# Writing out the loops of four engines as straight code in a two-layer transformer trunk

## What is computed

```python
for l in range(DEPTH):                                   # DEPTH = 2
    need_ctx = l < DEPTH - 1
    mod  = silu(c)     @ w_mod[l] + b_mod[l]             # 6 rows of 1024
    modc = silu(c_ctx) @ w_mod[l] + b_mod[l]
    h, hc = modulated rms_norm of x, of xc
    p = (h or hc) @ w_in[l]                              # q, k, v, gates of three mixers
    y = sigmoid(g0) * (retention(p) @ w_ret_o) \
      + sigmoid(g1) * (latent_attention(p) @ w_mla_o) \
      + sigmoid(g2) * (grouped_attention(p) @ w_gqa_o)
    x = x + mod[2] * (y @ w_out)
    h2 = modulated rms_norm of x
    a, b = split(h2 @ w_ffn_in[l]);  x = x + mod[5] * ((silu(a) * b) @ w_ffn_out[l])
    # the same for the context stream xc, only where need_ctx
return rms_norm(x, g_final)
```

## Time and profile before

| | before |
|---|---|
| runs | 3406.63, 3413.54, 3417.59 us; median 3413.54 |
| the profiled execution | 3408.35 us, its span 3406.2 us |
| instructions in the trace | 49718 |
| TensorE matmul busy | 3200.3 us (94%), 18760 matmuls |
| VectorE, ScalarE, GpSimd busy | 44%, 36%, 12% |
| loads of function tables on ScalarE | 96, of 1.283 us each |
| mean granted TensorE clock | 0.977 of full speed |

### The profile page before, as it was taken

One profiled execution on the slowest core, in us unless ns is written; L12 is line 12 of the kernel. 1 busy time (PEld: TensorE's weight loads), 2 busy tenths in 40 slices (PEclk: granted clock), 3 DMA queues, 4 the chain that ended last, 5 costly groups with the idle time before them and its releaser, 6 DMA issues.

```text
span 3406.2 us, 49718 instructions
## 1 busy us (share of the span) xinstructions
PE 3200.3 (94%) x18760; PEld 2716.6 (80%) x18760; DVE 1512.8 (44%) x2047; ACT 1241.8 (36%) x1777; POOL 397.4 (12%) x304
## 2 busy tenths in 40 slices
PE   6999999999999989999999988998999899899998
PEld 5788888899888878788888867887788787678886
DVE  5555524454436533422222255554455456443334
ACT  3344432444434432221211234444355444432222
POOL 0011100111102201000100100111011112010001
PEclk9999999999999999999999988999999999899999
DMA  4222132111242243123232332222222242322222
GB/s 187 75 70 73 68 124 76 63 62 60 76 150 66 67 139 128 55 91 119 68 122 88 123 124 85 76 73 82 89 76 73 73 133 81 118 80 99 93 98 99
DMA packets 100921, 315.17 MB, mean 93 GB/s; under 512 B 11088, under 2 KB 21456, under 8 KB 100816
## 3 DMA queue, kind: packets, MB, share of 16 engines
q1 hardware_dynamic: 55872, 202.40, 18.0%
q10 hardware_dynamic: 44944, 111.32, 9.7%
HBM read 283.79 MB, written 29.88 MB: 92 GB/s over the span
## 4 chain that ended last, share of the span: by engine, by line
PE 52%; DVE 4%; issue 3%; ACT 2%; POOL 0%; DMA 0%; ACTq 0%; DVEq 0%; POOLq 0%
PE ps L1443 49%; PE ps L1531 1%; PE ps L1558 1%; DVE wl L921 1%; ACT wh L441 0%; POOL ptl L1425 0%; DVE tmp L931 0%; DVE hl L1096 0%; PE ps L1572 0%; DVE tmp L1087 0%; DMA xz<-xspill 0%; PE ps L1467 0%; ACT prob L492 0%; ACTq L674 0%; PE ps L1501 0%
## 5 line engine op out<-in xcount | busy, mean ns | idle before, releaser
L1443 PE MATMUL ps<-hh,wh 128*128 128x512 f32 x2768 | 831.7, 361 | 35.3 <-DVE wl L921 15.5
L1443 PE MATMUL ps<-hh,wl 128*128 128x512 f32 x2768 | 814.0, 354 | 0.0
L1443 PE MATMUL ps<-hl,wh 128*128 128x512 f32 x2768 | 813.5, 354 | 0.0
L921 DVE TENSOR_TENSOR wl<-raw,wh 128x1024 fp32r<-128x1024 f32 x364 | 489.0, 1344 | 515.3 <-ACT wh L441 486.4
L1443 PEld LDWEIGHTS ps<-hh,wh 128*128 128x128 f32 x2768 | 452.8, 190 | 119.0 <-issue 34.3
L1443 PEld LDWEIGHTS ps<-hh,wl 128*128 128x128 f32 x2768 | 451.8, 190 | 76.4
L1443 PEld LDWEIGHTS ps<-hl,wh 128*128 128x128 f32 x2768 | 452.5, 190 | 74.3 <-issue 0.7
L441 ACT ACTIVATE wh<-raw 128x1024 fp32r<-128x1024 f32 x364 | 383.2, 1054 | 216.5 <-PE ps L1443 181.5
L1443 PE MATMUL ps<-yh,wh 128*128 128x512 f32 (+1 forms) x1296 | 408.8, 370 | 33.5 <-DVE wl L921 20.0
L1443 PE MATMUL ps<-yl,wh 128*128 128x512 f32 (+1 forms) x1296 | 396.1, 360 | 0.0
L1443 PE MATMUL ps<-yh,wl 128*128 128x512 f32 (+1 forms) x1296 | 395.7, 360 | 0.0
(11 more groups left out here) (192 smaller groups left out, 3407.5 us busy)
## 6 DMA issues: line engine op xcount, KB each, us to landing
raw<-in_stream SPq DMA_DIRECT2D x364, 512.0 KB, 3.5
prob<-in_wmod ACTq DMA_DIRECT2D x40, 512.0 KB, 3.5
mraw<-in_wmod ACTq DMA_DIRECT2D x36, 512.0 KB, 3.5
gspill<-prob ACTq DMA_DIRECT2D x32, 384.0 KB, 2.3
tmp<-gspill ACTq DMA_DIRECT2D x24, 384.0 KB, 3.2
early_y<-in_wmod SPq DMA_DIRECT2D x12, 512.0 KB, 14.2
vraw<-gspill ACTq DMA_DIRECT2D x16, 384.0 KB, 3.9
dec<-in_dec ACTq DMA_DIRECT2D x8, 768.0 KB, 4.2
```

What stands on the lines that cost most here:

```text
L921: dve.tensor_tensor(wl[:, s, :], raw[:, s, :], wh[:, s, :].bitcast(F32), ALU.subtract).then_inc(sem("w_lo"), 1)
L1443: ins = pe.matmul(out, lhs[w], rhs[x](cols), start=start and n == 0, stop=stop and n == 2)
```

## The change

Every `with engine.Fori(a, b) as i:` of TensorE, ScalarE, VectorE and GpSimd becomes `for i in range(a, b):`, a loop of the program that builds the kernel. The body is then emitted once a turn, with the turn's number as a constant in every wait and address. Nothing else is edited; order, operands and buffers are the same.

```diff
@@ scalar: attention
-                    with act.Fori(0, turns) as i:
+                    for i in range(0, turns):
                         t = At(ph, i)
                         for k in range(2):
                             attend(t, k, nt, scale(1 - k), home(kind, i, k + 1),
...
@@ scalar: merge
                     load_gate(at, 0, ph["g0"])
-                    with act.Fori(0, turns - 1) as i:
+                    for i in range(0, turns - 1):
                         turn(i)
                     turn(turns - 1, last=True)
...
@@ vector: merge
-                    with dve.Fori(0, turns) as i:
+                    for i in range(0, turns):
...
@@ gpsimd: ffn
-                    with pool.Fori(0, turns) as i:
+                    for i in range(0, turns):
...
@@ tensor: merge
                     turn(0, ph["begun"], late)
-                    with pe.Fori(1, turns) as i:
+                    for i in range(1, turns):
                         turn(i)
...
@@ tensor: out
-                    with pe.Fori(0, turns) as i:
+                    for i in range(0, turns):
                         t = At(ph, i)
```

More of the change, by code:

```diff
@@ L904, in _ @@
                         turn(0, paired=True)
-                    with act.Fori(1 if ph["paired"] else 0, turns) as i:
+                    for i in range(1 if ph["paired"] else 0, turns):
                         turn(i)
@@ L1293, in turn @@
                                               ALU.subtract).then_inc(sem("v_lo"), 1)
-                    with dve.Fori(0, turns - 1) as i:
+                    for i in range(0, turns - 1):
                         for h in range(2):
@@ L1355, in _ @@
                         turn(0, paired=True)
-                    with dve.Fori(1 if ph["paired"] else 0, turns) as i:
+                    for i in range(1 if ph["paired"] else 0, turns):
                         turn(i)
@@ L1402, in accumulate @@
                                            ALU.add).then_inc(sem("o_acc"), 1)
-                    with pool.Fori(0, turns - 1) as i:
+                    for i in range(0, turns - 1):
                         for k in range(2):
@@ L1876, in _ @@
                         turn(0, paired=True)
-                    with pe.Fori(1 if ph["paired"] else 0, turns) as i:
+                    for i in range(1 if ph["paired"] else 0, turns):
                         turn(i)
```

4 lines of the change are left out of this document (1 added, 3 removed).

## The result

| | before | after |
|---|---|---|
| median of the runs | 3414.09 us (6 runs, 3406.63 to 3417.59) | 3395.67 us (6 runs, 3389.17 to 3398.19) |
| ratio | | 0.9943, 95% interval 0.993 to 0.9956 |
| the profiled execution's span | 3406.2 us | 3394.4 us |
| instructions in the trace | 49718 | 45616 |
| loads of function tables | 96 | 64 |

The straight code is 18.4 us faster, 0.57%. The interval of the ratio makes that 15 to 24 us. The prediction said 3397.0 (3385 to 3410) and faster.

The account below looks back on a forecast made before the run. TensorE's matmuls, busy 94%, were taken as the bound, so savings count only in its 206 us of idle time. 8.7 + 3 + 3 + 2 + 0 = 16.7, say 17 us, off 3413.54 gives 3397 us, range 3385 to 3410.

Parts of the forecast that it names:

- Part 1: ScalarE's table loads at loop heads go, 32 in all; six at merge beginnings are on TensorE's path: 8.7 us, bounds 0 to 11.
- the two ways in: A table load stands at a loop's head where entry and the body's own end leave different tables; 18 at L441.
- the draining of 1.38 us: The skill's extra per table switch, 2.66 us together, would make the merge saving at most 16 us; not used in the sum.
- Part 2: TensorE's half-clock stretches behind three of six merge beginnings, 6.2 us together; one or two go: 3 us, bounds 0 to 6.2.
- a clock that falls as often as before: Sign of being wrong in the changed kernel's profile; alone it would bring the saving to 14 us.
- Part 3: In attention loops VectorE starts `yl` 0.12 us sooner behind `yh`, 22 waits, plus ScalarE register steps: 3 us, bounds 0 to 6.
- Part 4: TensorE's branches at 12 turn ends of out phases with modulation rows: 2 us, bounds 0 to 4.
- The idle row of 0.16 us: TensorE's "issue" wait after the small fold matmuls, before the next out-phase turn's first matmul; 12 such turn ends, 2 us.
- Part 5: TensorE's straight code fetches 130 to 150 instruction blocks instead of 72, without idling: 0 us.
- Rival B: Instruction blocks come too late; TensorE stands still 0.8 us for each of some 70 more: 56 us slower, 3453. Chance 0.07.
- Rival C: Each of TensorE's 60 branches back costs a 0.8 us fetch today, so 48 us more would go: 3349. Chance 0.04.
- Rival A: The table loads stay, or their saving is taken up: 3408.5 us, no measurable change. Chance 0.17.

Follow-up runs that it names:

- peel: Kernel before, all loops kept, with only ScalarE's first turn of each merge written out ahead of its loop: 3403.24 us, ratio 0.9957.
- merge_loops: Changed kernel with only ScalarE's merge loop put back as a loop: 3402.27 us, ratio 0.9968 to the kernel before.
- four_loads: Changed kernel plus four unused one-element instructions (Silu, Sqrt, Silu, Sqrt) ahead of each merge's first split, 24 more table loads: 3438.11 us, ratio 1.0068 to the kernel before.
- act_only: Kernel before with only ScalarE's loops written out: 3397.34 us, ratio 0.9956.
- dve_only: Kernel before with only VectorE's loops written out: 3409.81 us, ratio 0.999.
- pe_only: Kernel before with only TensorE's loops written out: 3410.02 us, ratio 0.9989.
- loop_warm: Kernel before, all loops kept, plus a one-element Exp by ScalarE behind the square root of grouped attention's norm: 3401.63 us, ratio 0.996.

## Why the prediction was right

**What bounds it.** That the main part lies with ScalarE's tables was right: ScalarE alone brings 0.44% of the 0.57%. That the change can't pay on TensorE itself wasn't quite: its loops alone bring 0.11% (0.01 to 0.22). The 1.6 us of "issue" in the list of waits didn't show that.

**Part 1, the loads at the head (8.7 us).** The six gaps shrank by 8.5 us. The number of loads was right to the unit: 64, none at L441 and L797, six at L769. peel and merge_loops show that the rule is the two ways in, and four_loads that a load at this place costs its full length. Where I said that the draining of 1.38 us which the Trainium skill (page "ScalarE: Activation LUTs", section "What ACT_TABLE_LOAD costs") adds to a switch isn't in this trace, four_loads agrees. There a load follows the instruction before it after 0.01 to 0.05 us, and load and instruction repeat every 1.50 us.

**Part 2, the clock (3 us, 0 to 6.2).** It can be read at the places: the merge columns add up to 10.1, 12.0 and 10.4 us where the loads are gone (after, act_only, peel), and the gaps shrank by 8.5, 8.7 and 9.8 us. So 1.6, 3.3 and 0.6 us are the clock's at the merges, and 3 was in the upper part of what came. It lies where it was expected: the columns of merges 2, 3 and 6, behind which the clock had been low, are 1.6, 1.2 and 1.7 us above what their gaps lost, 4.5 together; half-clock stretches inside the columns of merges 1 and 4 take part of it back. These are the stretches of the earlier trace rows after the change:

```profile
935.00:938.40 3.40, 2.61 (x16) 2.04 (x15) 1.23 (x1) 1.89 (x2) 0.00 (x0) 1.00 0.95 340
1201.90:1205.30 3.40, 3.40 (x12) 2.89 (x12) 2.28 (x4) 1.00 (x2) 0.00 (x0) 0.50 1.00 390
2907.00:2912.00 5.00, 3.12 (x14) 2.35 (x13) 3.35 (x4) 4.21 (x5) 0.00 (x0) 1.00 0.59 184
```

The second merge's start is at full clock, the third's low stretch is 3.4 instead of 6.8 us, the sixth's is gone. But the sign that I had named against this part, a clock that falls as often as before, is also there: 22 stretches before and 22 after, 155.4 and 160.0 us. Others came elsewhere, and over the whole profile of after nothing is left of this part. (The totals are counted to the end of the execution.) Over all the profiles of this case this total lies between 133.5 and 166.1 us (four_loads apart) with no order that follows the edits. One profile's total says nothing about so small a change; the places do.

**Part 3, the waits of attention loops (3 us).** Oversized. The hand-over to `yl` is 0.12 us shorter, as said, but the gap of TensorE, which waits for it, shrank by 0.03 only. The same place in dve_only (the first two rows) and in pe_only (the next two) shows why:

```profile
2591.08 0.42 DVE L978 TENSOR_TENSOR yl<-ps,yh 128x256 fp32r<-128x256 f32 x1 [1.71 <-ACT yh L501]
...
2591.56 0.62 PE L1443 MATMUL ps<-k2h,q2h 128*128 128x512 f32 x2 [1.28 <-DVE yl L978]
```

```profile
2586.46 0.42 DVE L978 TENSOR_TENSOR yl<-ps,yh 128x256 f32 x1 [1.84 <-ACT yh L501]
...
2587.03 0.59 PE L1443 MATMUL ps<-k2h,q2h 128*128 128x512 f32 x2 [1.48 <-DVE yl L978]
```

With VectorE's loops alone written out (the first pair) the gap falls by all of it, from 1.41 to 1.28 us. With TensorE's alone (the second pair) it grows: TensorE starts 0.15 us after the end of `yl` (2586.46 + 0.42 to 2587.03), where in a loop it starts after 0.06 (2591.08 + 0.42 to 2591.56). The changed kernel has both, some 0.12 us less and 0.09 more, so 1.38 us. The prediction saw only the first of the two. Why TensorE starts later there isn't shown.

The time of a head hardly moved: in layer 0's latent attention 40.70 us before and after, in layer 1 35.77 and 35.63, and in the grouped attention there 30.75 and 30.62. In layer 0's grouped attention it is 39.65 and 39.51, but loop_warm, with all its loops, has 39.51 there too. All that is some 2.5 us at most. dve_only, which has only VectorE's share, shows 1.0 us in layer 1's grouped attention and 0.10% in all, which isn't told from nothing.

**Part 4, TensorE's branches (2 us, 0 to 4).** Undersized. The idle row of 0.16 us is gone:

```profile
1546.00 0.38 PE L1572 MATMUL ps<-sel,tmp 128*128 128x2 f32 x2 [0.40 <-ACT tmp L600]
1546.24 0.60 PE L1443 MATMUL ps<-yh,wh 128*128 128x512 f32 x2
```

But a turn is shorter by more than that row. The turns of the first two phases take 21.22 to 21.33 us before and 21.00 or 21.01 after, those of the third 17.03 to 17.10 and 16.77 or 16.78. These lengths go with TensorE's program alone: pe_only and merge_loops have 21.01, and act_only, dve_only and peel, where TensorE keeps its loops, 21.22 to 21.33. That is about 0.3 us at each of the 12 ends, some 3.5 us, near the upper bound. The idle row is only the part that lies behind the fold matmuls; where the rest lay before (with small matmuls the ends are modelled) the trace doesn't show.

**Part 5, what is added (0).** Right, with 150 blocks for the 130 to 150. Between 260 and 418 us, where there was no instruction queue, it now reads:

```profile
q8 instruction: 7, 0.11, 0.3%
```

Rival B falls with it. Rival C fell too. The 60 branches back are gone, and with pe_only the gain is 4 us, not 48. A turn of the latent attention in layer 0 is some 3.6 blocks long (an estimate: 7 blocks in 158 us, 81.4 us a turn), and no block came when it branched back. The Trainium skill (page "Runtime: NRT & Kernel Launch", section "Instruction fetch mechanics") states that a taken branch out of the two-page window has to fetch its target first. The trace speaks against that for these bodies only if the window is two blocks of 16 KB also on TensorE; the same section gives TensorE a buffer of 128 KiB, and such a body would fit in that. The runs don't tell the two apart. Rival A fell in the compiled program: the loads went.

By place, in the profile of after, part 1 came out at 8.5, part 2 at 1.6, part 3 at no more than 2.5, part 4 at 3.5: 16.1 us at most, for the predicted 16.7. The spans of the two profiles differ by 11.8 and the medians by 18.4, with 15 to 24 from the interval. So the mechanism of the main part is shown, and the total is confirmed only to within some 4 us. That the forecast met the median within 1.3 us is partly luck: parts 3 and 4 missed in opposite directions, and the clock's part was real at its places and lost elsewhere.

## What to carry to other kernels

Look at where function tables are loaded: a load ahead of an instruction that needs no table, as often as a loop has turns, tells that the loop is entered with one table and comes back with another. One turn written out ahead of it removes the load as well as full unrolling does; and where a load must stay, a one-element instruction of the coming function, placed where the engine is idle, takes it off the path. Here this brought 13.7 us with all loops kept and 18 to 21 us on top of the unrolling (each good to some 5 to 9 us), as much as all the unrolling (18.4); by place it was 9.9 and 11.7 us. Whether such a load matters is read from the gap of the engine that waits, at that place: of the 18 loads at the split's line 12 went without a gain.

## What the runs showed of the hardware that I had not expected

- A few microseconds of stall cost more than their length: 24 loads with their instructions, 1.50 us each (36 us), lengthened TensorE's gaps by 33.6 us and the merges by 42.5 us by place (42.4 by the medians, good to 8), with 27.6 us more at half clock.
- An unrolled TensorE program that fetches twice the instruction blocks (150 to 72, 2.46 to 1.18 MB) isn't slower, and an end of a turn with small matmuls was dearer in the loop (about 0.3 us) than its idle row showed (0.16 us).
- Straight code doesn't shorten every hand-over. VectorE started 0.04 instead of 0.16 us after ScalarE's copy, but TensorE 0.15 instead of 0.06 us after VectorE's result.
- The time at half clock scatters from profile to profile of kernels that differ little (133.5 to 166.1 us, worth 16 us), which is a good part of what hid effects of a few microseconds here.
